# Gate products of a PEER layer from bf16 one-hots in three gate parts, four groups in three slabs

## The reference

```python
q = (xb @ w_pq).reshape(PEER_BLOCK, P_HEADS, 2, P_HALF)
sc = jnp.einsum('thpc,hpkc->thpk', q, sub_keys)
sv, si = lax.top_k(sc, TOPK)                       # 16 of 128 keys, twice a head
cand = (sv[..., 0, :, None] + sv[..., 1, None, :]).reshape(PEER_BLOCK, P_HEADS, TOPK * TOPK)
cid = (si[..., 0, :, None] * N_KEYS + si[..., 1, None, :]).reshape(PEER_BLOCK, P_HEADS, TOPK * TOPK)
fv, fi = lax.top_k(cand, TOPK)
eid = jnp.take_along_axis(cid, fi, axis=-1)        # expert = row * 128 + column
g = jax.nn.softmax(fv.astype(jnp.float32), axis=-1).astype(xb.dtype)
ue = jnp.take(u_experts, eid, axis=0)
ve = jnp.take(v_experts, eid, axis=0)
a = jax.nn.gelu(jnp.einsum('thkd,td->thk', ue, xb), approximate=False)
return jnp.einsum('thk,thkd->td', g * a, ve)
```

## Time and profile before

| | us |
|---|---|
| runs | 2204.07, 2201.74, 2202.97; median 2202.97 |
| the profiled execution | 2208.66, its span 2207.0 |
| TensorE busy | 2152.3 (98% of the span) |
| VectorE busy | 1683.5 (76%) |
| ScalarE busy | 1098.2 (50%) |
| GpSimd busy | 367.5 (17%) |

### The profile page before, as it was taken

One profiled execution on the slowest core, in us unless ns is written; L12 is line 12 of the kernel. 1 busy time (PEld: TensorE's weight loads), 2 busy tenths in 40 slices (PEclk: granted clock), 3 DMA queues, 4 the chain that ended last, 5 costly groups with the idle time before them and its releaser, 6 DMA issues. The chain is left out here.

```text
span 2207.0 us, 46403 instructions
## 1 busy us (share of the span) xinstructions
PE 2152.3 (98%) x14712; PEld 2005.6 (91%) x14712; DVE 1683.5 (76%) x2461; ACT 1098.2 (50%) x1651; POOL 367.5 (17%) x344
## 2 busy tenths in 40 slices
PE   6999999999999999999989999999999999999998
PEld 6999899999999988888889989999999998888886
DVE  6665658999999687677775746599999996667776
ACT  6445454444444454554464545444444445554454
POOL 3110110000000155334230101100000002333442
PEclk9999999999999999999998999999999999999999
DMA  5444466765555677777644444567655557777774
GB/s 192 153 144 152 145 207 213 230 203 178 173 174 176 224 260 242 239 242 243 223 135 135 150 166 168 188 225 231 194 175 176 171 176 256 244 240 242 241 240 164
DMA packets 173982, 437.49 MB, mean 198 GB/s; under 512 B 19360, under 2 KB 84896, under 8 KB 172752
## 3 DMA queue, kind: packets, MB, share of 16 engines
q1 hardware_dynamic: 173232, 432.09, 59.5%
q0 software_dynamic: 672, 4.39, 0.6%
HBM read 399.70 MB, written 36.70 MB: 198 GB/s over the span
## 5 line engine op out<-in xcount | busy, mean ns | idle before, releaser
L746 DVE TENSOR_TENSOR w_lo<-raw,w_hi 128x1024 fp32r<-128x1024 f32 x680 | 844.7, 1245 | 401.8 <-ACT w_hi L714 183.1
L1143 PE MATMUL ps<-act_hi,w_hi 128*128 128x256 f32 x2880 | 829.6, 288 | 3.2 <-DVE act_lo L797 1.9
L1143 PE MATMUL ps<-act_lo,w_hi 128*128 128x256 f32 x2880 | 819.8, 285 | 0.0
L1143 PE MATMUL ps<-act_hi,w_lo 128*128 128x256 f32 x2880 | 819.8, 285 | 0.0
L1143 PEld LDWEIGHTS ps<-act_hi,w_hi 128*128 128x128 f32 x2880 | 558.1, 194 | 5.5 <-DVE act_lo L797 2.3
L1143 PEld LDWEIGHTS ps<-act_hi,w_lo 128*128 128x128 f32 x2880 | 558.2, 194 | 0.1
L1143 PEld LDWEIGHTS ps<-act_lo,w_hi 128*128 128x128 f32 x2880 | 557.5, 194 | 0.0
L714 ACT ACTIVATE w_hi<-raw 128x1024 fp32r<-128x1024 f32 x248 | 263.1, 1061 | 323.5 <-PE ps L1403 311.7
L1403 PE MATMUL ps<-w_hi,act_hi 128*128 128x512 f32 x1000 | 389.2, 389 | 2.0 <-DVE act_lo L1107 2.0
L1403 PE MATMUL ps<-w_lo,act_hi 128*128 128x512 f32 x1000 | 389.0, 389 | 0.0
L1403 PE MATMUL ps<-w_hi,act_lo 128*128 128x512 f32 x1000 | 389.0, 389 | 0.0
(11 more groups left out here) (248 smaller groups left out, 2105.9 us busy)
## 6 DMA issues: line engine op xcount, KB each, us to landing
raw<-slabs SPq DMA_DIRECT2D x684, 512.0 KB, 3.6
h_park<-h_out SPq DMA_DIRECT2D x256, 128.0 KB, 1.7
h_in<-h_park SPq DMA_DIRECT2D x250, 128.0 KB, 3.7
memT<-mem POOLq DMA_DIRECT2D x2, 1024.0 KB, 6.6
skT<-sub_keys POOLq DMA_DIRECT2D x2, 1024.0 KB, 8.0
x_park<-xT SPq DMA_DIRECT2D x2, 1024.0 KB, 5.4
xT<-x_park SPq DMA_DIRECT2D x2, 1024.0 KB, 8.4
xT<-x SPq DMA_DIRECT2D x1, 1024.0 KB, 5.0
```

Source lines behind the costliest of these rows:

```text
L746: nc.vector.tensor_tensor(w_lo[:, j].rearrange("p k c -> p (k c)"), raw[:, j, :], w_hi[:, j].rearrange("p k c -> p (k c)").bitcast(FP32), ...
L1143: last = nc.tensor.matmul(ps[:, j, 0:T], w[:, j, k, :], a[:, k, :], start=(k == 0 and i == 0), stop=(k == KB - 1 and i == 2))
```

## The change

The one-hots become bf16 with four tokens innermost. The ramp `iota` is stored as bf16 with each number four times, and `hot_col`, `row_is` and `hot_row` have the shape keys x 4 tokens in place of 4 tokens x keys, so the broadcasts over keys lie in the middle. The row and column keys and the gate are kept as bf16 in `picks`; the gate now in three parts, each the rest of those before rounded to bf16. A group has twelve matmuls in place of eight, their operands taken at a step of four elements, 8 bytes.

The gates start at slab 76 instead of 60 and take 48 slabs: four groups in three slabs, placed by `GATES_AT` ahead of chunk 0 and chunk 6 of the first slab, chunk 4 of the second and chunk 2 of the third. The transposes stand ahead of slab 74 instead of 58, and ScalarE's exponential comes after 60 U slabs instead of 48.

```diff
@@ -92,12 +92,17 @@
 WHOLE = 2
 GROUPS = T // 4
-HOT_AT = 60
-RET_AT = 58
-EXP_AT = 48
-TAIL_AT = HOT_AT + GROUPS
+HOT_AT = 76
+RET_AT = 74
+EXP_AT = 60
+BODY = 12
+GATES_AT = (((0, 0), (1, 6)), ((2, 4),), ((3, 2),))
+BODY_GROUPS = BODY // 3 * 4
+TAIL_AT = HOT_AT + GROUPS // BODY_GROUPS * BODY
 EARLY = RING - 1
 H_SLOTS = 2
+PARTS = 3
 TEMPS = 88
 LO_EVERY = 1.9
...
-        hot_col = at("hot_col", x_at, [P, 4, P], F32R)
-        hot_row = at("hot_row", x_at + 2048, [P, 2, 4, P], F32R)
+        hot_col = at("hot_col", x_at, [P, P, 4], BF16)
+        hot_row = at("hot_row", x_at + 2048, [P, PARTS, P, 4], BF16)
         h_out = at("h_out", x_at + 6144, [P, H_SLOTS, T])
         early_hi = at("early_hi", x_at, [P, EARLY, T], F32R)
         early_in = at("early_in", x_at + EARLY * T * 4, [P, EARLY, T])
...
-        iota = sb("iota", [P, P])
+        iota = at("iota", top[0], [P, P, 4], BF16)
+        top[0] += P * 4 * 2
         cand_at = sb("cand_at", [P, TOPK])
         par_at = top[0]
...
         wif_hi = sb("wif_hi", [P, KB, 8], F32R)
         wif_lo = sb("wif_lo", [P, KB, 8], F32R)
...
+        row_is = at("row_is", par_at, [P, P, 4], BF16)
         assert top[0] - par_at >= 4 * P * 2
-        rowT = sb("rowT", [P, T])
-        colT = sb("colT", [P, T])
-        gate2 = sb("gate2", [P, 2, T], F32R)
+        picks = at("picks", top[0], [P, 2 + PARTS, T], BF16)
+        top[0] += (2 + PARTS) * T * 2
         gated_at = top[0]
         gate = sb("gate", [P, NKEYS, T])
...
-            nc.gpsimd.iota(iota[:], [[1, P]], base=0, channel_multiplier=0,
+            nc.gpsimd.iota(iota[:], [[1, P], [0, 4]], base=0, channel_multiplier=0,
                            allow_small_or_imprecise_dtypes=True).then_inc(consts, 1)
             pool.dma_start(par[:], params[0]).then_inc(par_loaded, 16)
...
-                with act.Fori(0, GROUPS // RING) as g:
-                    for s in range(RING):
-                        gelu_out(HOT_AT - (0 if s else RING), g, (s - 1) % RING)
-                        act.wait_ge(gate_mm, layer * GROUPS + g * RING + s + 2)
-                        settle(act)
-                        nc.scalar.activation(gate[:, :, ds(g * (4 * RING) + 4 * s, 4)],
-                                             ps[:, 4 + s, :].rearrange("p (t i) -> p i t", t=4),
-                                             ACT.Copy).then_inc(gate_copied, 1)
+                with act.Fori(0, GROUPS // BODY_GROUPS) as g:
+                    for s in range(BODY):
+                        gelu_out(HOT_AT - (0 if s else RING), g * (BODY // RING) + max(s - 1, 0) // RING, (s - 1) % RING)
+                        for i, _ in GATES_AT[s % 3]:
+                            n = s // 3 * 4 + i
+                            act.wait_ge(gate_mm, layer * GROUPS + g * BODY_GROUPS + n + 2)
+                            settle(act)
+                            nc.scalar.activation(gate[:, :, ds(g * (4 * BODY_GROUPS) + 4 * n, 4)],
+                                                 ps[:, 4 + i, :].rearrange("p (t i) -> p i t", t=4),
+                                                 ACT.Copy).then_inc(gate_copied, 1)
                 gelu_out(TAIL_AT - RING, 0, RING - 1)
...
-                step.mark(nc.vector.tensor_copy(rowT[:], ps[:, 4, 0:T]))
-                step.mark(nc.vector.tensor_copy(colT[:], ps[:, 4, T:2 * T]))
-                step.link(nc.vector.tensor_copy(gate2[:, 0], ps[:, 5, 0:T]))
-                step.link(nc.vector.tensor_tensor(gate2[:, 1], ps[:, 5, 0:T], gate2[:, 0].bitcast(FP32), ALU.subtract))
+                step.mark(nc.vector.tensor_copy(picks[:, 0:2], ps[:, 4, :].rearrange("p (i t) -> p i t", i=2)))
+                step.link(nc.vector.tensor_copy(picks[:, 2], ps[:, 5, 0:T]))
+                step.link(nc.vector.tensor_tensor(g_rest[:], ps[:, 5, 0:T], picks[:, 2], ALU.subtract))
+                step.link(nc.vector.tensor_copy(picks[:, 3], g_rest[:]))
+                step.link(nc.vector.tensor_tensor(picks[:, 4], g_rest[:], picks[:, 3], ALU.subtract))
                 dve.wait_ge(x_parked, layer * 16 + 16)
                 for j in range(2):
                     lo_part(layer, U_AT + HOT_AT, 0, j)
...
                     settle(dve)
-                    nc.vector.tensor_tensor(row_is[:], iota[:].unsqueeze(1).to_broadcast([P, 4, P]),
-                                            rowT[:, ds(n * 4, 4)].unsqueeze(2).to_broadcast([P, 4, P]),
+                    nc.vector.tensor_tensor(row_is[:], iota[:],
+                                            picks[:, 0, ds(n * 4, 4)].unsqueeze(1).to_broadcast([P, P, 4]),
                                             ALU.is_equal).then_inc(row_is_ready, 1)
                     dve.wait_ge(gate_mm, layer * GROUPS + n + 1)
                     dve.wait_ge(row_is_ready, layer * GROUPS + n + 1)
                     settle(dve)
-                    nc.vector.tensor_tensor(hot_col[:], iota[:].unsqueeze(1).to_broadcast([P, 4, P]),
-                                            colT[:, ds(n * 4, 4)].unsqueeze(2).to_broadcast([P, 4, P]),
+                    nc.vector.tensor_tensor(hot_col[:], iota[:],
+                                            picks[:, 1, ds(n * 4, 4)].unsqueeze(1).to_broadcast([P, P, 4]),
                                             ALU.is_equal).then_inc(hot_col_ready, 1)
-                    nc.vector.tensor_tensor(hot_row[:], row_is[:].unsqueeze(1).to_broadcast([P, 2, 4, P]),
-                                            gate2[:, :, ds(n * 4, 4)].bitcast(FP32).unsqueeze(3).to_broadcast([P, 2, 4, P]),
+                    nc.vector.tensor_tensor(hot_row[:], row_is[:].unsqueeze(1).to_broadcast([P, PARTS, P, 4]),
+                                            picks[:, 2:2 + PARTS, ds(n * 4, 4)].unsqueeze(2).to_broadcast([P, PARTS, P, 4]),
                                             ALU.mult).then_inc(hot_row_ready, 1)
-                with dve.Fori(0, GROUPS // RING) as g:
-                    for j in range(RING):
-                        hot_rows(g * RING + j)
-                        lo_part(layer, U_AT + HOT_AT + (j + 2) // RING * RING, g, (j + 2) % RING)
+                with dve.Fori(0, GROUPS // BODY_GROUPS) as g:
+                    for n in range(BODY_GROUPS):
+                        hot_rows(g * BODY_GROUPS + n)
+                        if n % 4 < 3:
+                            ahead = n // 4 * 3 + n % 4 + 2
+                            lo_part(layer, U_AT + HOT_AT, g * (BODY // RING) + ahead // RING, ahead % RING)
                 for j in (2, 3):
                     lo_part(layer, U_AT + TAIL_AT, 0, j)
...
                     for i in range(4):
-                        for part in range(2):
-                            last = nc.tensor.matmul(ps[:, 4 + s, i * P:(i + 1) * P], hot_col[:, i, :],
-                                                    hot_row[:, part, i, :], start=(part == 0), stop=(part == 1))
+                        for part in range(PARTS):
+                            last = nc.tensor.matmul(ps[:, 4 + s, i * P:(i + 1) * P], hot_col[:, :, i],
+                                                    hot_row[:, part, :, i], start=(part == 0), stop=(part == PARTS - 1))
                     last.then_inc(gate_mm, 1)
-                with pe.Fori(0, GROUPS // RING) as g:
-                    for j in range(RING):
-                        gates_of(g * RING + j, j)
-                        pe.wait_ge(lo_ready[j], lo_count(layer, U_AT + HOT_AT, g))
-                        pe.wait_ge(act_evac, layer * ACT_EVS + (U_EV + HOT_AT) + g * RING + j + 1)
-                        slab_product(j, act_hi, act_lo)
+                with pe.Fori(0, GROUPS // BODY_GROUPS) as g:
+                    for s in range(BODY):
+                        j = s % RING
+                        def gates_before(k):
+                            for i, at_k in GATES_AT[s % 3]:
+                                if k == at_k:
+                                    gates_of(g * BODY_GROUPS + s // 3 * 4 + i, i)
+                        pe.wait_ge(lo_ready[j], lo_count(layer, U_AT + HOT_AT, g * (BODY // RING) + s // RING))
+                        pe.wait_ge(act_evac, layer * ACT_EVS + (U_EV + HOT_AT) + g * BODY + s + 1)
+                        slab_product(j, act_hi, act_lo, gates_before)
                 group(layer, U_AT + TAIL_AT, U_EV + TAIL_AT)
```

More of the change, by code:

```diff
@@ L182, in trunk @@
         wif_lo = sb("wif_lo", [P, KB, 8], F32R)
-        row_is = at("row_is", par_at, [P, 4, P], BF16)
+        row_is = at("row_is", par_at, [P, P, 4], BF16)
         assert top[0] - par_at >= 4 * P * 2
-        rowT = sb("rowT", [P, T])
-        colT = sb("colT", [P, T])
-        gate2 = sb("gate2", [P, 2, T], F32R)
+        picks = at("picks", top[0], [P, 2 + PARTS, T], BF16)
+        top[0] += (2 + PARTS) * T * 2
         gated_at = top[0]
@@ L262, in trunk @@
         struck = tmp("struck", 109, [P, 2, NKEYS])
+        g_rest = tmp("g_rest", 104, [P, T])
```

(2 more changed lines are left out.)

## The result

The changed kernel took 2262.89 us (median of 4 runs, 2262.26 to 2264.61), the kernel before 2203.52 in the same comparison: a ratio of 1.0266, interval 1.0247 to 1.0286. The forecast was 2195 with a range up to 2238. It is slower, by 59 us.

What follows compares the result with a forecast made beforehand. TensorE and VectorE were both taken as full in the gate stretch, at one pace. Terms -7.5 + 0.3 - 0.5 - 7.0 + 6.4 = -8.3 us took 2203.0 to about 2195; range 2176 to 2238.

Steps and rivals of the forecast that it cites:

- The gate block itself: TensorE's gate matmuls: twelve bf16 at 0.061 us a step, 0.835 us against 0.89, 128 times: -7.0 us (bounds -15, +63).
- The first rival: TensorE's gate matmuls: stepped bf16 weights load no faster, 0.111 us a matmul, +63 us, total 2258; chance 0.12.
- The decode: TensorE's transposes, moved from slab 58 to 74, no longer wait for VectorE's g_exp: -7.5 us over two layers.
- the near miss at slab 62: VectorE waits 4.3 us for the exp; w_lo ready at 497.3, TensorE wants it at 497.4: +0.3 us.
- The first block: From the transposes to a layer's first gates: 7.55 us in both layers, against 7.96 and 7.64: -0.5 us.
- VectorE's rate: Gate stretch: two bf16 elements per cycle; row_is and hot_col 0.43 us, hot_row 0.955 us.
- The new wait: VectorE's w_lo waits for w_hi, delaying every fourth gate block about 0.2 us per three slabs: +6.4 us (0 to +13).
- The end of the block: Last gate matmul to the product on TensorE: step stays 0.114 us ahead of an fp32r load, plus 0.05 at product's head.
- The third rival: TensorE's gate matmuls: shorter load not fully overlapped, 0.08 to 0.09 us a matmul, +20 to +34, about 2222; chance 0.12.

Runs made afterwards that it cites:

- the pairs: Changed kernel with two tokens innermost instead of four, moving operand at a step of 4 bytes, hot_row made by two operations: 2191.86 us, ratio 0.9945.

## Why the prediction was wrong

**The step that failed is "The gate block itself".** It took 0.061 us for a step, on the ground that 0.11 was the load of 4-byte weights and that with half the bytes a load would hide under its matmul. The load did shrink, 192 to 117 ns, and would have set no pace: with a dense moving operand the steps are 0.056, next to the 0.055 that I had as the lower bound. But 0.061 had been read from a matmul with a dense moving operand, and the change gives it a step of 8 bytes. I weighed that step for the weights only and for VectorE's operands, never for the moving columns. The term was -7.0 us; it measured 128 x 0.53 = +68, just past my upper bound of +63, and the moving operand made the difference (2262.2 against 2191.8 with it dense). With both operands dense a block costs 0.65 + 0.08 = 0.73: 128 x -0.16 = -20.5, the decode and first blocks -8, the new wait (below) +14, together -14.5. Measured were 2187.1 against 2205.6 in that comparison, -18.5. The 4 us that the sum lacks are not traced; the runs' mean clocks, 0.994 to 0.996 against 0.992 to 0.994, may hold a part.

**The first rival** gave 2258 with a chance of 0.12. It had the right place, and the right price by luck: its cause, the load, was wrong, and the moving operand's step happens to cost nearly the same, 0.118 a matmul against the 0.111 that it put on the load. Its "no row has strided weights or columns" named the gap; an operand form that no row shows should have had more chance than "half the bytes" left it. The range left it out.

**The decode** was right: the wait gone, -7.5 us, the near miss at slab 62 without a gap (4.38 us waited on VectorE, 4.3 forecast). **The first block** was right: 7.54 us from the transposes in both layers, 7.55 forecast. **VectorE's rate** was right in all three operations.

**The new wait** was real but mis-sized. In the changed kernel it stands on VectorE alone, 0.56 us, as the slow blocks hide it:

```profile
612.80 1.23 DVE L755 TENSOR_TENSOR w_lo<-raw,w_hi 128x1024 fp32r<-128x1024 f32 x1 [0.56 <-ACT w_hi L669]
```

With quick blocks it stands at TensorE. With both operands dense the fourth block starts 0.49 to 0.65 us behind the last product matmul (605.48 ahead of this row) instead of 0.12:

```profile
605.97 0.84 PE L1393 MATMUL ps<-hot_row,hot_col 128*128 128x128 bf16 x12 [0.21 <-DVE hot_row L1103]
```

That is 0.43 a unit on average, and 0.5 in the pairs, where I had 0.2, with 0.4 as the upper bound: 14 to 16 us, not 6.4. About 0.1 of it is the shorter block, which brings TensorE there earlier. The end of the block was off the other way: the step from the last gate matmul to the product is 0.03 to 0.05, not the 0.114 that I gave it, and the product's head costs 0.08 instead of 0.05. Why is not shown; the product's first matmul has a record of 0.37 us in place of 0.28, so it may have started ahead of its weights.

The third rival had 0.08 to 0.09 a step, and 0.081 is the back-to-back figure of the Trainium skill (TensorE: Matmul & The Clock Gate, Back-to-back issue gap). No run with a dense moving operand shows such a gap: it is 0.056 with a load for each matmul. The fast weight load of the Trainium skill (TensorE: Matmul & The Clock Gate, Weight-path perf modes), at about twice the speed and with stepped weights allowed, agrees: the records are 98 ns for dense and 113 for stepped bf16 weights, 192 for 4-byte ones.

## What to carry to other kernels

Look at the step of the moving operand of each matmul that a new layout touches: on bf16, 128 columns at 8 bytes cost 0.118 us, and at 4 bytes 0.057, as much as dense. A layout with two values innermost kept VectorE's doubled rate and TensorE's pace alike, where four had only the first. And when an operand's form is new, a duration from a row with another form is a bound and not the value: its upper end deserves a chance of its own.

## What the runs showed of the hardware

- A moving operand of bf16 at steps of 2, 4, 6, 8 and 16 bytes: 0.056, 0.057, 0.090, 0.118 and 0.231 us for 128 columns at the full clock.
- Weights of bf16 at a step of 8 bytes: the load's record is 113 ns, 98 dense; the pace is 0.056 us in both. Under a moving operand with a step of 8 bytes dense weights show 115 ns, so the record follows the matmuls' pace too.
- Twelve bf16 matmuls with a load each run at 0.056 us a step; eight of 4-byte operands at 0.11 to 0.12.
- Behind a block of matmuls at 0.231 us a step the granted clock was 0.57 over 3.7 us, though TensorE was busy throughout by its records; the whole execution had a mean of 0.963. It didn't follow every block, and the cause is open.
